# Latent attention's queries and keys as high and low parts, rotated keys first

## What is computed

```python
def queries(cq, rot):
    q = (rms_norm(cq, q_norm_g) @ w_uq).reshape(bn, l, C_HEADS, C_NOPE + C_ROPE)
    return q[..., :C_NOPE], rot(q[..., C_NOPE:])
def keys(kv_part, rot):
    ckv, kr = jnp.split(kv_part, [C_KV_LORA], axis=-1)
    kv = (rms_norm(ckv, kv_norm_g) @ w_ukv).reshape(bn, l, C_HEADS, C_NOPE + C_VDIM)
    return kv[..., :C_NOPE], rot(kr), kv[..., C_NOPE:]
...
s = jnp.einsum('bqhd,bkhd->bhqk', qn_b, kn) + jnp.einsum('bqhd,bkd->bhqk', qr_b, kr)
p = jax.nn.softmax(s.astype(jnp.float32) * scale, axis=-1).astype(v.dtype)
return jnp.einsum('bhqk,bkhd->bqhd', p, v)
```

## Time and profile before

| | before |
|---|---|
| median of 3 runs | 1611.78 us (1611.52 to 1611.93) |
| the profiled execution's own time | 1612.91 us |
| its span in the trace | 1610.9 us |
| mean granted TensorE clock | 0.978 |
| PE busy share of the span | 95% |

### The profile page before, as it was taken

The page is one execution under the profiler, slowest core; times in us unless marked ns, Lnnn a source line. Parts: engine busy times, 40 slices in busy tenths (PEclk is TensorE's granted clock), DMA queues, the critical chain, the costliest instruction groups (busy, mean ns, idle before and its releaser), DMA issues.

```text
span 1610.9 us, 31037 instructions
## 1 busy us (share of the span) xinstructions
PE 1530.0 (95%) x11614; PEld 1360.3 (84%) x11614; DVE 1130.3 (70%) x1875; ACT 793.4 (49%) x1433; POOL 113.4 (7%) x134
## 2 busy tenths in 40 slices
PE   7999988899899999999899999999999889999998
PEld 6788877797688888878786799999998669999997
DVE  7986866544899888888645478875675756577653
ACT  4545562423545445322555567765435445666542
POOL 0000242412000000010000000001000001000000
PEclk9999998999899999999899999999999999999999
DMA  9355410003344454565431046566544214255552
GB/s 373 109 187 180 171 43 1 4 1 105 118 170 158 166 171 168 190 222 201 165 107 53 22 148 188 185 192 211 178 158 131 92 53 158 92 185 189 185 184 91
DMA packets 62878, 229.75 MB, mean 143 GB/s; under 512 B 6849, under 2 KB 8129, under 8 KB 62401
## 3 DMA queue, kind: packets, MB, share of 16 engines
q1 hardware_dynamic: 61616, 222.65, 41.0%
q0 software_dynamic: 1168, 5.80, 1.0%
HBM read 227.38 MB, written 1.05 MB: 142 GB/s over the span
## 4 chain that ended last, share of the span: by engine, by line
PE 83%; DVE 9%; ACT 4%; issue 3%; DMA 0%; DVEq 0%; POOL 0%; ACTq 0%; SPq 0%; POOLq 0%
PE proj L696 23%; PE proj L698 22%; PE proj L697 22%; DVE w_low L2304 1%; ACT w_high L1754 1%; PE bank L750 1%; PE bank L1011 1%; PE bank L1058 1%; PE bank L1028 1%; PE bank L758 1%; DVE mod_products L2408 1%; PE bank L1247 1%; PE proj L1232 1%; PE bank L1060 0%; PE proj L1233 0%
## 5 line engine op out<-in xcount | busy, mean ns | idle before, releaser
L696 PE MATMUL proj<-h_high,w_high 128*128 128x256 f32 (+1 forms) x1760 | 575.0, 327 | 14.8 <-DVE h_low L2338 6.4
L698 PE MATMUL proj<-h_high,w_low 128*128 128x256 f32 (+1 forms) x1760 | 564.5, 321 | 0.0
L697 PE MATMUL proj<-h_low,w_high 128*128 128x256 f32 (+1 forms) x1760 | 562.6, 320 | 0.0
L2304 DVE TENSOR_TENSOR w_low<-w_raw,w_high 128x1024 fp32r<-128x1024 f32 x320 | 390.3, 1224 | 140.7 <-ACT w_high L1754 139.5
L1754 ACT ACTIVATE w_high<-w_raw 128x1024 fp32r<-128x1024 f32 x320 | 335.2, 1053 | 234.2 <-PE proj L698 230.8
L696 PEld LDWEIGHTS proj<-h_high,w_high 128*128 128x128 f32 x1760 | 333.8, 190 | 47.2 <-issue 13.4
L698 PEld LDWEIGHTS proj<-h_high,w_low 128*128 128x128 f32 x1760 | 334.0, 190 | 26.5
L697 PEld LDWEIGHTS proj<-h_low,w_high 128*128 128x128 f32 x1760 | 333.5, 189 | 25.0
L696 PE MATMUL proj<-act_high,w_high 128*128 128x256 f32 (+1 forms) x608 | 190.6, 313 | 0.4 <-DVE w_low L2304 0.3
L698 PE MATMUL proj<-act_high,w_low 128*128 128x256 f32 (+1 forms) x608 | 189.8, 312 | 0.0
L697 PE MATMUL proj<-act_low,w_high 128*128 128x256 f32 (+1 forms) x608 | 189.2, 311 | 0.0
(11 more groups left out here) (434 smaller groups left out, 1954.2 us busy)
## 6 DMA issues: line engine op xcount, KB each, us to landing
w_raw<-w_stream SPq DMA_DIRECT2D x322, 512.0 KB, 3.4
a_ring<-a_stream SPq DMA_DIRECT2D x80, 512.0 KB, 4.0
a_rows<-a_stream SPq DMA_DIRECT2D x8, 512.0 KB, 12.3
a_cols<-a_head SPq DMA_DIRECT2D x4, 1024.0 KB, 13.6
x<-x_in SPq DMA_DIRECT2D x1, 2048.0 KB, 8.7
late_tab<-late_tables POOLq DMA_DIRECT2D x1, 1408.0 KB, 6.7
cond_rows<-cond_rows POOLq DMA_DIRECT2D x1, 1024.0 KB, 5.0
x<-mem_in POOLq DMA_DIRECT2D x1, 1024.0 KB, 5.9
```

The source lines that it names most:

```text
L696: mm(out_, wh, xh, start=first, stop=False)
L697: mm(out_, wh, xl, start=False, stop=False)
L698: return mm(out_, wl, xh, start=False, stop=last)
L2304: v.tensor_tensor(wl(n), RAW[:, n % 4, :], wh(n), ALU.subtract).then_inc(w_low, 1)
```

## The change

The plain queries, the plain keys and both rotated parts are kept as a high and a low part in float32r, and a score is three products of these parts instead of one product of float32 numbers.

- For query tiles 0 to 7 and all 8 key tiles, ScalarE's copy out of the bank is the high part (it raises `qk_high`), and VectorE subtracts it from the bank to get the low part (`qk_low`); that subtraction now raises `tile_out` and frees the bank.
- VectorE's queue is written out anew: the `low` of weight blocks, the `qk_low` and the chunks of the norms `ckv` and `mem` stand in one order. The spread of the norm factor `ckv` on TensorE moves from behind query tile 2 to behind tile 4.
- `ROPE1` has the key first. After each rotation ScalarE copies the high part of the rotated tile (`rope_parts`, among the copies of `ukv_v`) and VectorE subtracts the low part. TensorE no longer waits for all rotations ahead of the attention; each pair of heads waits for its own rotated low part between the plain and the rotated products.
- Places in SBUF are shared anew so that the parts fit.

```diff
-        ROPE1 = [(MQ[:, 8 + i, :], T0["uq"] + 8 + i, "m") for i in range(4)] + [(KR[:, LAT], T0["in1"] + 5, "m")]
+        ROPE1 = [(KR[:, LAT], T0["in1"] + 5, "m")] + [(MQ[:, i, :], T0["uq"] + 8 + i, "m") for i in range(4)]
+        ROPE1_PARTS = [(KR[:], KRH[:], KRL[:])] + [(MQ[:, i, :], MRH[:, i, :], MRL[:, i, :]) for i in range(4)]
...
-            chunks("uq", 3, CQH, CQL, "cq", lambda m: norm_spread("ckv") if m == 2 else None)
+            chunks("uq", 3, CQH, CQL, "cq", lambda m: norm_spread("ckv") if m == 4 else None)
...
-            pe.wait_ge(A["rp_d"], len(ROPE1))
...
-                for i, o in enumerate(banks):
-                    mm(o[:], MQ[:, h + i, q], KN[:, h + i, :], start=True, stop=False)
-                for i, o in enumerate(banks):
-                    mm(o[:], MQ[HALVES[i], 8 + h // 2, q], KR[HALVES[i], :], start=False, stop=True).then_inc(A["at_s"], 1)
+                nope = [(h_, k_) for h_, k_ in ((HH, KNH), (HH, KNL), (HL, KNH))]
+                for j, (qx, kx) in enumerate(nope):
+                    for i, o in enumerate(banks):
+                        mm(o[:], qx[:, h + i, SEQ + qt * P:SEQ + (qt + 1) * P], kx[:, h + i, :], start=(j == 0), stop=False)
+                pe.wait_ge(rope_low, 2 + h // 2)
+                for j, (qx, kx) in enumerate(((MRH, KRH), (MRH, KRL), (MRL, KRH))):
+                    for i, o in enumerate(banks):
+                        last = mm(o[:], qx[HALVES[i], h // 2, q], kx[HALVES[i], :], start=False, stop=(j == 2))
+                        if j == 2:
+                            last.then_inc(A["at_s"], 1)
...
-                        o = place_of(j)
-                        done(T0[name] + j)
-                        f(o, PL[(T0[name] + j) % 2][:, 0:o.shape[1]], ACT.Copy).then_inc(tile_out, 1)
+                        o, t = place_of(j), T0[name] + j
+                        done(t)
+                        if high and j < 8:
+                            f(o, PL[t % 2][:, 0:o.shape[1]], ACT.Copy).then_inc(qk_high, 1)
+                        else:
+                            if j == first:
+                                act.wait_ge(tile_out, t + 2)
+                            f(o, PL[t % 2][:, 0:o.shape[1]], ACT.Copy).then_inc(tile_out, 1)
...
+            def rope_parts(*some):
+                for i in some:
+                    act.wait_ge(A["rp_d"], i + 1)
+                    f(ROPE1_PARTS[i][1], ROPE1_PARTS[i][0], ACT.Copy).then_inc(rope_high, 1)
...
+            walk("ukv_v", lambda m: VT[:, m % 4, m // 4 * 512:(m // 4 + 1) * 512],
+                 lambda m: rope_parts(*{1: (0,), 3: (1,), 5: (2,), 6: (3,), 7: (4,)}.get(m, ())), first=0)
...
-            norm("ckv")
-            rest("uq")
-            norm("mem")
-            rest("ukv_k")
+            def qk_low(name, m):
+                t = T0[name] + m
+                hi, lo = (HH[:, m, LAT], HL[:, m, LAT]) if name == "uq" else (KNH[:, m, :], KNL[:, m, :])
+                dve.wait_ge(qk_high, m + 1 + (8 if name == "ukv_k" else 0))
+                v.tensor_tensor(lo, PL[t % 2][:, 0:hi.shape[1]], hi, ALU.subtract).then_inc(tile_out, 1)
+            events = [(DONE_BLOCK[B0["uq"] + b], 0, b) for b in range(5)] + [(DONE_TILE[T0["uq"] + t], 1, t) for t in range(8)]
+            for _, is_tile, j in sorted(events):
+                if not is_tile:
+                    low(B0["uq"] + j + lead("uq"))
+                elif j not in (4, 5):
+                    qk_low("uq", j)
+                if is_tile and j == 3:
+                    norm("ckv", lambda k: qk_low("uq", 4 + k))
+            def beside_mem(m):
+                qk_low("ukv_k", m)
+                if m == 3:
+                    low(B0["ukv_k"] + lead("ukv_k"))
+            norm("mem", beside_mem)
+            low(B0["ukv_k"] + 1 + lead("ukv_k"))
...
-            rotate(ROPE1, 0, range(len(ROPE1)))
+            rotate(ROPE1, 0, range(2))
+            rope_parts(0)
+            rotate(ROPE1, 0, (2,))
+            rope_parts(1)
+            rotate(ROPE1, 0, (3,))
+            rope_parts(2)
+            rotate(ROPE1, 0, (4,))
+            rope_parts(3, 4)
             rest("ukv_v")
```

More of the change, by code:

```diff
@@ L429, in two_blocks_kernel @@
         late = cursor[0]
+        KR = place("kr", [P, T2])
+        MQ = place("mla_q", [P, 4, SEQ])
+        MRH = place("mla_rope_high", [P, 4, SEQ], F32R)
+        MRL = place("mla_rope_low", [P, 4, SEQ], F32R)
+        KNH = place("mla_k_high", [P, 8, T2], F32R)
+        VT = place("mla_v", [P, 4, 1024])
+        CKH = place("ckv_high", [P, 2, T2], F32R)
+        CKL = place("ckv_low", [P, 2, T2], F32R)
+        cq_at = cursor[0]
         CQ = place("cq", [P, 3, SEQ])
         CKV = place("ckv", [P, 2, T2])
[L432 to L435, removed]
         CQH = place("cq_high", [P, 3, SEQ], F32R)
         CQL = place("cq_low", [P, 3, SEQ], F32R)
-        CKH = place("ckv_high", [P, 2, T2], F32R)
-        CKL = place("ckv_low", [P, 2, T2], F32R)
+        after_cq = cursor[0]
+        cursor[0] = cq_at
+        KNL = place("mla_k_low", [P, 8, T2], F32R)
+        assert cursor[0] >= after_cq
+        KRH = place("kr_high", [P, T2], F32R)
+        KRL = place("kr_low", [P, T2], F32R)
         cursor[0] = late
@@ L536, in two_blocks_kernel @@
         dn_scaled = sem("dn_scaled")
+        qk_high, rope_high, rope_low = sem("qk_high"), sem("rope_high"), sem("rope_low")
         mix_gain, mix_rows = sem("mix_gain"), sem("mix_rows")
@@ L588, in two_blocks_kernel @@
         CTX = slice(0, SEQ)
-        ROPE1 = [(MQ[:, 8 + i, :], T0["uq"] + 8 + i, "m") for i in range(4)] + [(KR[:, LAT], T0["in1"] + 5, "m")]
+        ROPE1 = [(KR[:, LAT], T0["in1"] + 5, "m")] + [(MQ[:, i, :], T0["uq"] + 8 + i, "m") for i in range(4)]
+        ROPE1_PARTS = [(KR[:], KRH[:], KRL[:])] + [(MQ[:, i, :], MRH[:, i, :], MRL[:, i, :]) for i in range(4)]
+        assert cursor[0] <= end
         QI, KI, WI, LAT_KV, QR, KRP, QB, KB, QN = 0, 4, 5, 6, 7, 9, 10, 14, 18
@@ L2112, in _, with walk @@
             norm_root("ckv")
-            def walk(name, place_of, beside=None):
+            def walk(name, place_of, beside=None, high=None, first=False):
                 nb, nt = next((b, t) for s, b, t in STAGES if s == name)
@@ L2134, in beside_uq @@
                         square("mem", k, (mem_ready, 16))
-            walk("uq", lambda m: MQ[:, m, :], beside_uq)
+            walk("uq", lambda m: HH[:, m, LAT] if m < 8 else MQ[:, m - 8, :], beside_uq, True, 8)
             norm_root("mem")
-            walk("ukv_k", lambda m: KN[:, m, :], lambda m: norm_high("mem", (m,)))
-            walk("ukv_v", lambda m: VT[:, m % 4, m // 4 * 512:(m // 4 + 1) * 512])
+            walk("ukv_k", lambda m: KNH[:, m, :], lambda m: norm_high("mem", (m,)), True)
+            walk("ukv_v", lambda m: VT[:, m % 4, m // 4 * 512:(m // 4 + 1) * 512],
+                 lambda m: rope_parts(*{1: (0,), 3: (1,), 5: (2,), 6: (3,), 7: (4,)}.get(m, ())), first=0)
             def attend(ly, out_bank, out_chunks):
@@ L2822, in _, with rope_parts @@
             dve.wait_ge(n_lo, NORM_S0["mem"] + KC)
-            rotate(ROPE1, 0, range(len(ROPE1)))
+            def rope_parts(*some):
+                for i in some:
+                    x, hi, lo = ROPE1_PARTS[i]
+                    dve.wait_ge(rope_high, i + 1)
+                    v.tensor_tensor(lo, x, hi, ALU.subtract).then_inc(rope_low, 1)
+            rotate(ROPE1, 0, range(2))
[6 more added lines that the diff above has]
+            rope_parts(3, 4)
             rest("ukv_v")
```

## The result

The changed kernel takes 1618.57 us in the median (1615.69 to 1619.83, 6 runs) beside 1611.72 us before (1610.24 to 1612.19, 6 runs). The medians lie 6.9 us apart; the ratio taken over the runs is 1.0036 with an interval of 1.0024 to 1.0047, which puts the cost of the change at some 5.8 us (3.9 to 7.6). I had forecast 1613.8 us and most likely no difference that can be measured. The median lies 1.0 us above the upper end of my range (1617.6 us).

A forecast was written before the change was run, and what follows sets the result against it. TensorE, busy 95% of the span, was taken as the bound. The terms -3.3 + 3.4 + 2.0 - 0.55 + 0.4 = +2.0 us gave a median of 1613.8 us (chance 0.5), with a range from 1610.2 to 1617.6 us.

The forecast's parts named there:

- The clock: Rival, chance 0.25: TensorE's clock falls to half in `uq`, tiles 8 to 11, costing 0.3 to 2 us: 1615.5 us.
- Scores, -3.3 us: Attention: a period falls from 5.89 to 5.35 us; six pairs at 0.55 us less each give -3.3 us.
- 0.86 if the heads overlap: Attention scores: a pair's rotated float32r products take 0.86 us if the two heads overlap, 1.47 if not.
- Banks of `uq`, +3.4 us: `uq`: TensorE's waits for VectorE's subtractions sum to 6.2 us against 2.8 before, +3.4 us, between 2.0 and 4.5.
- tile 9: `uq`: waits 1.8 us for tile 7's subtraction, behind eight squares, a ScalarE block and the same block on VectorE.
- Banks of `ukv_k`, +2.0 us: `ukv_k`: longer bank rounds and a block after tile 3 cost +2.0 us over eight tiles, between 1.0 and 3.0.
- The wait behind the block after tile 3: `ukv_k`: tile 6 waits 1.1 us for a block put in after tile 3 on VectorE.
- Start of the attention, -0.55 us: Attention's start: 0.3 us gained at the first transpose and 0.25 more at the second, -0.55 us.
- nearly all hidden: Attention's start: removing the 1.31 us rotated-key wait gains little; VectorE's first maximum still follows its two weight blocks.
- Restarts, +0.4 us: New TensorE waits: slower first products, 0.22 instead of 0.118 us, some eight, half on the path, +0.4 us.
- my own signs of being wrong: `uq` passed without these waits, clock dropping before 838 us, or stretches behind 915 us changing over a few tenths.
- the evacuation is hidden: Rival, chance 0.15: VectorE's blocks fall where TensorE has other work; both bank terms cost some 2 us, not 5.4: 1610.4 us.

The follow-up runs named there:

- the scores alone: The kernel before with three-product float32r scores of high parts only, low parts left out: 1606.38 us, ratio 0.9966.
- the order altered: The changed kernel, two banks, with squares of `mem` behind tile 7, subtractions ahead of blocks, and one block behind the norm: 1611.75 us, ratio 1.000.
- idle products: The changed kernel with 6, 13, 6 and 18 unread TensorE products ahead of query tiles 4, 7, 8 and 9: 1616.90 us, ratio 1.0024.
- the late blocks: The changed kernel with VectorE's last two weight blocks behind steps 4 and 6 of the attention: 1616.13 us, ratio 1.0022.
- four banks and the old order: The changed kernel with four PSUM banks in turn instead of two for `uq` and `ukv_k`, queues unchanged: 1615.37 us, ratio 1.0020.
- order and late blocks: The changed kernel, two banks, with the order altered and the late blocks: 1611.74 us, ratio 0.9989; with four banks added 1606.64 us, 0.9958, and 1604.54 us, 0.9953.

## Why the prediction failed

The sign and the size of the terms at full clock were about right. The clock was mis-sized, by the most, and with it the answer that most likely no difference can be measured.

- **Scores, -3.3 us.** The step "0.86 if the heads overlap" held: 0.90 us for a rotated pair in float32r. The Trainium skill's rule that products on distinct row groups run concurrently (TensorE: Matmul & The Clock Gate, Part 3: Packing small matmuls) is borne out here for this format. The records of a pair do start by twos, at 889.60, 889.94 and 890.17 us. The records of before are 0.43 us apart and not 0.45, which leaves 0.21 us for filling and emptying and would have given the 0.90. The plain products take 1.56 us where I had 1.47, and the period is 5.39 where I had 5.35. Mis-sized was the count, six pairs here and two put down as nearly hidden: all eight pairs gain, 3.9 us, as the scores alone show; the changed kernel gets 2.9 of them at full clock (46.05 beside 48.97).
- **Banks of `uq`, +3.4 us.** Put down tile by tile, the waits were 1.0, 0.3, 2.0, 1.0 and 1.8 us (6.1, which I rounded to 6.2). Measured, as the gap between starts less 0.118 us, they are 0.92, 0.30, 1.82, 0.90 and 2.50: 6.4 us, and 2.6 before. That is +3.9. The step that missed is tile 9: I left out that ScalarE waits for `ckv`'s last low part before the squares (the 0.72 us behind the row of 827.40), and it carries through to 832.56.
- **Banks of `ukv_k`, +2.0 us.** Measured +2.4, of which 0.4 is clock. The wait behind the block after tile 3 is 0.80 where I had 1.1.
- **Start of the attention, -0.55 us.** In the change the first maximum comes 18.07 us after the last product of `ukv_k` (857.84 to 875.91), before 18.11, so "nearly all hidden" held there. But the reason given was incomplete. The 3.2 us from the first block to the first maximum that I carried over hold 0.86 us of idle time, which goes with the wait: alone it is worth 1.0 us. The change loses that again to the two rotated low parts ahead of the blocks. `ukv_v` is 0.7 us shorter, and the attention gives 1.0 us back to the blocks; both parts together are 3.6 us at full clock (0.7 and 2.9), where I had 3.85.
- **Restarts, +0.4 us.** Of the 5.8 us by which `uq` grew, 3.9 are gaps and 1.5 clock; the 0.4 left is what this term says.
- **The clock.** This was a rival of 0.25 with 0.3 to 2 us and stood at nothing in the sum, and it is the step that failed. Two of my own signs of being wrong came: the clock dropped before 838 us (at 832.9), and what lies behind 915 us grew by 0.8. In the profiled execution it costs 1.5 us in tiles 9 to 11 (832.56 to 837.38 is 4.82 us, 27 products at 0.118 and a slow first one are 3.3), 1.0 in the sums of `mem` (6.34 beside 5.33), 0.4 in `ukv_k` and 1.6 in the attention (47.64 beside 46.05): 4.5 us. I priced the first item alone, and took the 1.00 from 825 to 830 us with two waits as evidence against it. That the attention's start, with two waits of 1.18 and 0.73 us, could lose the clock I did not consider.

Without these 4.5 us the stretch would have grown by 2.7 us, beside a forecast of 2.0. That is one execution. Over all of them the mean granted clock is 0.974 in the six of the change, 0.977 in 85 of the kernel before beside the experiments, and 0.977 again in the 12 with the order altered. With the two levels that is some 9 us more at half clock in an execution of the change, which costs at most half of it, 4.7 us (an estimate). So the clock is a share of the loss in the other executions too, and 4.5 us is near the most that it can be there. That the clock follows the waits is shown for `uq` (idle products hold it at 1.00); for the attention it is argued from executions with and without the late blocks, not shown by a run that changes the clock alone.

The rival "the evacuation is hidden" failed on the ground I named, the written-out order. The runs show the order to be the larger cause: with it alone altered all 5.8 us are back, clock included, with four banks and the old order 2.6. The Trainium skill's advice to clear PSUM with both ScalarE and VectorE (TensorEngine Tiling (Array Packing), PSUM Bottleneck) is not tested here, as one bank passes through both engines in turn and no version gives them different banks.

## What to carry to other kernels

When a second engine joins the clearing of a PSUM bank, go through its queue and ask of each instruction ahead of the clearing whether someone waits for it sooner; here swapping three places in the queues was worth as much as the change lost, the clock's share included. Price each new wait of TensorE twice, once as its own length and once as the work behind it at half clock, and do so at every place where waits stand close together. More banks are a gain of their own: here 2.6 us with the old order and with the new one, though within the noise each time, and 5.8 us with order and late blocks.

## What the hardware showed beyond that

The clock fell without a long idle stretch: the longest wait ahead of 832.9 us in the change is 2.34 us, and ahead of the fall at 829.4 us with the altered order it is 1.67 us, with 2.56 us of 5 busy. Yet from 825 to 830 us the changed kernel kept 1.00 with 2.59 us busy. The kernel before itself spread from 1608.57 to 1615.09 us over 24 runs on one chip. Which stretches ran at half clock differs from one profiled execution to the next, in unchanged code as well (793.6 to 797.0 us is at half in before and not in after, which is at half until 788.5 us where before rises at 786.8). A term of the clock should therefore be given as a range, and one profiled execution not be taken for it.
